# Weight pieces split in place: six high slots, low parts over the raw piece, clearing spread over the dense stage

## Time and profile before

| what | value |
|---|---|
| median of three runs | 1771.09 us (1769.48 to 1774.81) |
| the profiled execution's own time | 1762.26 us |
| its span, first to last instruction | 1760.5 us |
| mean granted TensorE clock | 0.980 |
| TensorE busy | 1648.9 us |
| VectorE busy | 1357.8 us |
| ScalarE busy | 1022.7 us |
| moved by DMA | 526.64 MB, 299 GB/s on average |

### The profile page before, as it was taken

One profiled execution on the slowest core, in us unless ns is written; L12 is line 12 of the kernel. 1 busy time (PEld: TensorE's weight loads), 2 busy tenths in 40 slices (PEclk: granted clock), 3 DMA queues, 4 the chain that ended last, 5 costly groups with the idle time before them and its releaser, 6 DMA issues.

```text
span 1760.5 us, 20788 instructions
## 1 busy us (share of the span) xinstructions
PE 1648.9 (94%) x7272; PEld 1275.6 (72%) x7273; DVE 1357.8 (77%) x1147; ACT 1022.7 (58%) x824; POOL 69.7 (4%) x85
## 2 busy tenths in 40 slices
PE   6999897999999998999999989999899999999995
PEld 2587756888587765777877768888677777787773
DVE  5687765775797776889888886565588888888888
ACT  1375432334266433778777775545577877777773
POOL 1200030000100001000000000000000000000200
PEclk9999998999999998999999999999999999999998
DMA  9885459874496445999999996666699999999992
GB/s 365 308 317 186 144 190 394 320 273 148 166 341 220 148 168 192 394 396 371 393 374 356 395 384 226 215 221 213 217 369 388 375 395 395 391 388 341 389 393 109
DMA packets 217236, 526.64 MB, mean 299 GB/s; under 512 B 9889, under 2 KB 14161, under 8 KB 217185
## 3 DMA queue, kind: packets, MB, share of 16 engines
q1 hardware_dynamic: 208770, 496.15, 77.1%
q0 software_dynamic: 8336, 29.55, 4.6%
q10 hardware_dynamic: 80, 0.26, 0.0%
HBM read 518.85 MB, written 15.47 MB: 304 GB/s over the span
## 4 chain that ended last, share of the span: by engine, by line
PE 78%; DVE 10%; issue 5%; DMA 3%; ACT 2%; ACTq 0%; DVEq 0%; SPq 0%
PE ps L1535 19%; PE ps L1537 19%; PE ps L1536 18%; PE ps L1541 5%; PE ps L1542 4%; DVE w_lo L1391 4%; PE ps L1546 4%; DMA w_raw<-in_ffn_w_dram 2%; PE ps L2036 2%; PE ps L2067 1%; DMA w_raw<-in_w_mod_mix_dram 1%; PE ps L1576 1%; ACT w_hi L814 1%; DVE gates L1170 1%; DMA w_raw<-in_w_in_dram 1%
## 5 line engine op out<-in xcount | busy, mean ns | idle before, releaser
L1391 DVE TENSOR_TENSOR w_lo<-w_raw,w_hi 128x2048 fp32r<-128x2048 f32 x333 | 756.5, 2288 | 173.4 <-ACT w_hi L814 171.1
L814 ACT CAST w_hi<-w_raw 128x2048 fp32r<-128x2048 f32 x333 | 633.6, 1910 | 178.9 <-PE ps L1542 86.9
L1535 PE MATMUL ps<-w_hi,actT_hi 128*128 128x512 f32 (+1 forms) x1464 | 583.2, 398 | 48.0 <-DVE w_lo L1391 17.3
L1537 PE MATMUL ps<-w_hi,actT_lo 128*128 128x512 f32 (+1 forms) x1464 | 569.0, 389 | 0.0
L1536 PE MATMUL ps<-w_lo,actT_hi 128*128 128x512 f32 (+1 forms) x1464 | 568.3, 388 | 0.0
L1535 PEld LDWEIGHTS ps<-w_hi,actT_hi 128*128 128x128 f32 x1464 | 278.1, 190 | 123.7 <-issue 35.0
L1537 PEld LDWEIGHTS ps<-w_hi,actT_lo 128*128 128x128 f32 x1464 | 277.8, 190 | 57.6
L1536 PEld LDWEIGHTS ps<-w_lo,actT_hi 128*128 128x128 f32 x1464 | 278.6, 190 | 53.9 <-issue 1.7
L954 DVE TENSOR_TENSOR w_lo<-w_raw,w_hi 128x2048 fp32r<-128x2048 f32 x81 | 185.4, 2289 | 104.0 <-ACT w_hi L551 103.7
L551 ACT CAST w_hi<-w_raw 128x2048 fp32r<-128x2048 f32 x81 | 154.5, 1908 | 132.4 <-PE ps L1537 91.9
L1541 PE MATMUL ps<-w_hi,gT_hi 128*128 128x512 f32 x448 | 182.3, 407 | 8.6 <-DVE gT_hi L1418 5.4
(11 more groups left out here) (281 smaller groups left out, 1204.7 us busy)
## 6 DMA issues: line engine op xcount, KB each, us to landing
w_raw<-in_exp_w_dram SPq DMA_DIRECT2D x336, 1024.0 KB, 7.6
w_raw<-in_ffn_w_dram SPq DMA_DIRECT2D x33, 1024.0 KB, 5.4
w_raw<-in_w_mod_mix_dram SPq DMA_DIRECT2D x24, 1024.0 KB, 11.4
w_raw<-in_w_mod_ffn_dram SPq DMA_DIRECT2D x24, 1024.0 KB, 5.7
w_raw<-in_w_gate_dram SPq DMA_DIRECT2D x24, 1024.0 KB, 6.7
w_raw<-in_w_in_dram SPq DMA_DIRECT2D x14, 1024.0 KB, 6.4
w_raw<-in_w_out_dram SPq DMA_DIRECT2D x8, 1024.0 KB, 5.1
by_row<-constants_dram POOLq DMA_DIRECT2D x16, 512.0 KB, 18.4
```

The source lines that it names most:

```text
L814: nc.scalar.copy(w_hi[:, i % SPLIT, :], w_raw[:, i % RING, :]).then_inc(split_hi, 1)
L1391: TTn(w_lo[:, i % SPLIT, :], w_raw[:, i % RING, :], w_hi[:, i % SPLIT, :].bitcast(F32), ALU.subtract).then_inc(piece_used, 1)
L1535: MM(to, hi, w_h, start=first, stop=False)
L1537: return MM(to, lo, w_h, start=False, stop=last)
```

## The change

`w_lo` is declared over the same memory as `w_raw`, with six slots: the subtraction writes the low part over the raw piece. `w_hi` gets six slots (SPLIT = 6), so the memory for weights stays twelve slots. SyncE now loads into a slot when TensorE has used its piece (`split_used`), or VectorE its modulation piece. Three names take over the other meanings of SPLIT: UNSPLIT (raw pieces), LAG (how far events stand behind the casts in the streams) and LATE (the last pieces of the dense stage), all 3. The rings run on from stage to stage (`first_slot`, `slot()`).

In the expert loop ScalarE and VectorE treat one piece more ahead of each event; the fourth piece of the first expert is cast and subtracted before the loop. In one-block experts a gated panel is turned after the first piece of the next panel instead of after the third, into bank 6, and the next rows are turned behind the last gated panel, into banks 2 and 3, and released in two halves. GpSimd waits for `split_used` before each clearing DMA.

```diff
-RING, SPLIT = 6, 3
+RING, SPLIT = 6, 6
+UNSPLIT = 3
+LAG = 3
+LATE = 3
...
+    def slot(self, i):
+        return (self.first_slot + i) % RING
...
+def turned_bank(blocks, b):
+    return HW1 + 2 if blocks == 1 else HW1 + 2 * b
...
-TURN_EARLY, TURN_LATE = (6, 7), (5, 7)
+TURN_FREE, TURN_LATE = (2, 3), (5, 7)
...
-        w_raw = sb("w_raw", [P, RING, PIECE])
-        w_hi = sb("w_hi", [P, SPLIT, PIECE], F32R)
-        w_lo = sb("w_lo", [P, SPLIT, PIECE], F32R)
+        w_hi = sb("w_hi", [P, SPLIT, PIECE], F32R)
+        in_place = ExitStack()
+        w_lo = sb("w_lo", [P, RING, PIECE], F32R, scope=in_place)
+        in_place.close()
+        w_raw = sb("w_raw", [P, RING, PIECE])
...
-                    if i < RING:
-                        sp.wait_ge(piece_used, base + i + 1 + (gap if i < RING // 2 else 0))
-                    elif i < RING + stretch.raw:
-                        sp.wait_ge(split_used, split_base + i - RING + 1 + SPLIT)
-                    else:
-                        sp.wait_ge(piece_used, base + i + 1 - stretch.raw)
-                    load(i % RING, piece, mod_layer if piece[0] == "mod" else layer, expert)
+                    old = before.pieces[before.n - RING + i] if i < RING else stretch.pieces[i - RING]
+                    if old[0] == "mod":
+                        sp.wait_ge(piece_used, base + i + 1 - (0 if i < RING else stretch.raw))
+                    elif i < RING:
+                        sp.wait_ge(split_used, split_base + before.split_no[before.n - RING + i] - before.n_split + 1 + SPLIT)
+                    else:
+                        sp.wait_ge(split_used, split_base + stretch.split_no[i - RING] + 1 + SPLIT)
+                    load(stretch.slot(i), piece, mod_layer if piece[0] == "mod" else layer, expert)
...
                     for n in range(EXPERTS * TT):
+                        gp.wait_ge(split_used, MIX.n_split + 3 + 3 * n // 2 + SPLIT)
                         gp.dma_start(by_row[n * P:(n + 1) * P, :], consts[:, C_ZERO:C_ZERO + D]).then_inc(rows_cleared, 16)
...
-                            round_at(3, loads0, done0)
+                            round_at(4, loads0, done0)
                             gate_of(1, done0, panel_0, fold_0, first=True)
-                            round_at(4, loads0, done0)
                             round_at(5, loads0, done0)
+                            round_at(6, loads0, done0)
                             if packed:
                                 fold_up(3, done0)
-                            round_at(6, loads0, done0)
+                            round_at(7, loads0, done0)
                             def panel(loads, done, at, folds, last):
-                                round_at(7, loads, done)
+                                if blocks == 1:
+                                    gT_part(at)
+                                round_at(8, loads, done)
                                 gate_of(5, done, at, folds)
-                                round_at(8, loads, done)
-                                gT_part(at)
                                 round_at(9, loads, done)
+                                if blocks == 2:
+                                    gT_part(at)
+                                round_at(10, loads, done)
...
                                 pe.wait_ge(silu_ready, at)
-                                up(4, "A", 0, done)
+                                up(4, "A", 0, done, turn_previous if blocks == 1 else None)
                                 up(5, "A", 1, done)
                                 pe.wait_ge(gated_ready, at)
-                                up(6, "B", 0, done, turn_previous)
+                                up(6, "B", 0, done, turn_previous if blocks == 2 else None)
...
-                            if blocks == 1:
-                                with pe.If(e < EXPERTS - 1):
-                                    turn_rows(0, e + 1, TURN_EARLY)
-                                turn(panel_0 + NP)
...
+                            turn(panel_0 + NP)
+                            with pe.If(e < EXPERTS - 1):
+                                turn_rows(0, e + 1, TURN_FREE if blocks == 1 else TURN_LATE)
+                            with pe.Else():
+                                turn_places()
```

More of the change, by code:

```diff
@@ L141, with __init__ @@
 class Stretch:
-    def __init__(self, pieces, raw=0):
-        self.pieces, self.raw = pieces, raw
+    def __init__(self, pieces, raw=0, first_slot=0):
+        self.pieces, self.raw, self.first_slot = pieces, raw, first_slot
         self.loads, self.split_no = [], []
@@ L149, in __init__ @@
         for i, piece in enumerate(pieces):
-            landed[i % RING] += 32 if piece[0] == "branch" and piece[2] == 0 else 16
-            self.loads.append(landed[i % RING])
+            landed[self.slot(i)] += 32 if piece[0] == "branch" and piece[2] == 0 else 16
+            self.loads.append(landed[self.slot(i)])
             self.split_no.append(None if piece[0] == "mod" else n)
@@ L440, in _ @@
             for layer in range(DEPTH):
-                stream(MIX, layer * LAYER_PIECES + MOD0.n_used, layer, mod_layer=("ffn", layer), gap=layer * (RING // 2),
-                       split_base=layer * LAYER_SPLITS)
+                stream(MIX, layer * LAYER_PIECES + MOD0.n_used, layer, DENSE if layer else MOD0, layer * LAYER_SPLITS, mod_layer=("ffn", layer))
                 if layer < 1:
-                    stream(DENSE, MOD0.n_used + MIX.n_used, 0, mod_layer=("mix", 1), gap=RING // 2, split_base=MIX.n_split)
+                    stream(DENSE, MOD0.n_used + MIX.n_used, 0, MIX, MIX.n_split, mod_layer=("mix", 1))
                 else:
                     moe0 = MOD0.n_used + LAYER_PIECES + MIX.n_used
-                    sp.wait_ge(piece_used, moe0 + RING)
+                    assert [piece[0] for piece in MIX.pieces[-RING:]] == ["mod"] + ["branch"] + ["out"] * (RING - 2)
+                    sp.wait_ge(piece_used, moe0 - (RING - 1) + RING)
                     with sp.Fori(0, EXPERTS) as e:
-                        stream(EXPERT, e * EXPERT.n + moe0, 1, expert=e)
+                        stream(EXPERT, None, 1, EXPERT, e * EXPERT.n_split + LAYER_SPLITS + MIX.n_split, expert=e)
             for t in range(TT):
@@ L618, in route_norms @@
                 high_h(1)
+                ahead(3)
             act.wait_ge(c_loaded, 16)
@@ L953, in rest_of_piece @@
                 dve.wait_ge(split_hi, split_base + j + 1 - RAW_UP_TO.get(split_base, RAW_PIECES))
-                TTn(w_lo[:, j % SPLIT, :], w_raw[:, i % RING, :], w_hi[:, j % SPLIT, :].bitcast(F32),
+                slot = stretch.slot(i)
+                TTn(w_lo[:, slot, :], w_raw[:, slot, :], w_hi[:, (j - stretch.raw) % SPLIT, :].bitcast(F32),
                     ALU.subtract).then_inc(piece_used, 1)
@@ L1761, in project_raw @@
                         pe.wait_ge(hT_raw_ready, layer * 8 + 2 * t + i + 1)
[L1762 removed]
+                    slot = MIX.slot(i)
+                    pe.wait_ge(raw_loaded[slot], layer * (MIX.landed[slot] + DENSE.landed[slot]) + MOD0.landed[slot] + MIX.loads[i])
                     for k in range(4 * h, 4 * h + 4):
[L1764 removed]
+                        ins = raw_product(bank(2 * t + n % 2), k, t, slot, k % 4, BANK, k == 0, k == KD - 1)
                     return ins
[L1767 removed]
+                for i in range(UNSPLIT):
                     ins = project_raw(i, 0)
@@ L1775, in _ @@
                 second_tile(layer * 2, 0)
-                for i in range(SPLIT):
+                for i in range(UNSPLIT):
                     project_raw(i, 1).then_inc(split_used, 1)
                 for i, piece in enumerate(MIX.pieces):
-                    if piece[0] == "mod" or i < SPLIT:
+                    if piece[0] == "mod" or i < UNSPLIT:
                         continue
```

211 lines of the change are left out of this document (107 added, 104 removed).

## The result

The changed kernel takes 1758.3 us (median of four runs, 1755.7 to 1760.9) against 1771.2 before (four runs as well): ratio 0.993, interval 0.991 to 0.995. The gain is 13 us, less than half of the 31.5 forecast. The profiled execution took 1755.7 us (span 1753.8), against 1762.3 (1760.5) before, so between the two traces only 6.5 us are to be found.

A forecast was written before the change was run, and what follows sets the result against it. TensorE was busy 1648.9 of 1760.5 us, leaving 112 idle plus half-clock losses. Dense stage -15.0, experts -18, mixers +1.5 gave -31.5: profiled 1730.8, median 1739.6 us, range 1722 to 1761; forecast chance 0.62.

The forecast's parts named there:

- The view of the bound, and the clearing: Dense stage: the burst of clearings fills the DMA and stalls TensorE; spreading it gives -15.0 us, ends -10 and -16.
- Two signs: Dense stage: clearings land near 3 us each; a cast waiting over 3 us for a load would refute.
- The steady panel: Experts of few rows: with six slots the DMA sets the pace, a panel going from 16.33 to 16.0 us.
- the rival that feared for it: Split-weight ring too short: loads land late, all 35 panels lengthen; 1794 or 1822 us; chance of slower 0.09.
- the clearing still collides: Dense stage rival: spread clearings take back their gain, experts gain nothing; within 5 of 1771; no change 0.05.
- Six panels per such expert -2.0.: Experts of few rows: -0.33 us a panel, six panels, so -2.0 us in each of five experts.
- The boundary: Between experts: turning the last panel first, rows behind it, wins 1.0 us with few rows, 1.5 in two TensorE-bound experts.
- Around the experts' start: Ahead of the expert loop: one more cast and subtraction lie beside TensorE's "issue" gap; 0, at most +2.3 us.
- Mixers: Mixer stages: six slots are only three split pieces there, cover 1.3 us; +1.5 us for both layers, ends -2 and +10.
- dense stage only: Rival: DMA holds the expert stage, where nothing moves; gain 10 to 20, typically 15, so 1756 us; chance 0.22.

The follow-up runs named there:

- dense_only: The kernel before, with only the clearing of the row table spread over the dense stage; 1755.2 us, ratio 0.992.
- three: Changed kernel; first panel's product behind piece 4's low part, VectorE's loop head at slot 8, piece 2's low part before the gathered rows' wait; 1743.8 us.
- slot8: Changed kernel with the head of VectorE's expert loop at slot 8 of a code block instead of slot 0; 1754.4 us, ratio 0.991.
- dense_pad: Kernel before with the spread clearing and three increments of an unused semaphore ahead of VectorE's expert loop; 1760.7 us, ratio 0.995.
- held: Changed kernel with the first expert's loads of pieces 6 and up held until VectorE is in its expert loop; 1759.0 us, ratio 0.994.
- entry: Changed kernel with VectorE's loop head at slot 8 and piece 2's low part made before the gathered rows are waited for; 1749.8 us, ratio 0.990.
- gate_first: Changed kernel; in one-block experts the first panel's gated product comes behind piece 4's low part, not piece 6's; 1755.1 us, ratio 0.992.
- rest_only: Changed kernel with the sixteen clearings issued in one burst, as before; 1774.1 us, ratio 1.003.
- all_four: `three` plus the next rows turned ahead of the last panel in one-block experts; 1749.1 us, ratio 0.988.
- three_last: `three` with the last panel's gated product made before piece 10's low part in one-block experts; 1745.6 us, ratio 0.987.
- three_pe: `three` with the head of TensorE's expert loop at slot 0 of a block of its code; 1739.5 us, ratio 0.983.

## Why the prediction was wrong

*The view of the bound, and the clearing.* Right: -15.0 forecast for the stalled piece, -14.6 measured, and `dense_only` shows it as a gain of 14.6 in the median. Two signs were wrong, and nothing hung on them: a clearing lands in 6.9 us, not near 3, and casts there wait 3.3 and 4.6 us for a load, over the 3 us that were to refute the forecast, while TensorE waits for none of them.

*The steady panel.* Right in its mechanism: 16.0 us forecast, 15.95 in the chain of the third expert, DMA at 394 GB/s, ScalarE waiting for landings, landings of 6.9 to 9.4 us. By TensorE's count of pieces 10 to 39 a panel takes 15.6 to 15.7 us in the first, third, fifth and sixth expert (16.3 before), faster than forecast, and 16.3 in the last, as before. The ring is long enough; the rival that feared for it is refuted, and so is that the clearing still collides.

*"Six panels per such expert -2.0."* The third expert shows it (-1.9), and with its early waits gone in `three` it is no faster (113.97 us, from 113.69): there its panels take 15.9 instead of 15.7, so what it lost at piece 5 it had made up behind. The last expert is 3.5 us longer instead.

*The boundary, 1.0 and 1.5 us forecast.* Half right. The low part of the rows is off TensorE's path: the first piece behind the first, fifth and sixth expert is 1.7 us shorter. But 1.3 of the 1.7 go back at piece 40, so 0.4 of the 1.0 is left, and behind the third expert, whose successor's first piece is 0.8 longer, nothing. The full experts gain 0.9 of the 1.5, at piece 40 alone: the first piece behind them took 2.8 us before, too, so the 1.45 us were never there. I counted the eight transposes as moved beside other work; before, they themselves were what covered the product on VectorE. The last expert, with no next rows, loses 2.9 (piece 40 from 3.68 to 6.54), which the forecast has no term for.

*The step that failed: "Around the experts' start ... they lie beside it: 0, at most +2.3."* Its size was +13 at piece 4; the start being 3.3 earlier and later pieces making up 2, +7.4 is left for the first expert. I took TensorE's "issue" gap as the cover and asked only what one more subtraction costs. Two things were missing. VectorE's own entry into the loop, 8.0 us of standing before, has cover only as long as TensorE starts late, and whatever makes TensorE earlier uncovers it. And the entry's length isn't fixed: two more instructions ahead of a pinned loop head (6.5 us), and weight loads issued from 677.9 us on where the old ring had none between 684 and 698 (the rest: the second further jump took 5.0 us, from 2.4). `slot8` and `dense_pad` show the first, `held` the second (both further jumps were shorter in it, 1.1 and 3.7 us), and `entry` gets 5 to 8.5 us back.

*A term that was left out: the turn of the first panel moved up.* The diff puts it behind piece 4's products instead of piece 6's, and piece 6's low part in front of the product. The forecast spoke of the ring and of the last turn and never set this wait down. Piece 5 is longer by 15.3 us over six experts; 2.8 of it are the turns themselves, which only moved there, and 12.5 the wait and the slow clock behind it. Not all of that is lost time. `gate_first` won 5.8 us in experts 2 and 7, nothing in 3 and 8. From `entry` to `three` it is 6.0 us in the median, of which the traces have 4.1 in experts 2 and 7; a part of it may be the reload that `entry`'s trace has and `three`'s hasn't.

*Mixers, +1.5 forecast.* Near: piece by piece 0.7 and 0.45 us more. Another 1.4 us came ahead of the first split piece; that is scatter, since there the new ring's traces lie from 1.4 us under before's (`rest_only`) to 1.4 over (the changed kernel itself). Seven of the eleven with the new ring lose 1.4 us more in the first mixer, which this one doesn't; why was not tried. In the eleven traces with the new ring, the last piece before the stall ends at 281.6 to 284.0, in the three with the old one at 280.5 to 281.1.

*The rival "dense stage only"* is what was measured (1756 given, 1758.3 measured), for a reason that it did not name: the transfers did move, and waits of the change's own took it back. For the entry and for the first panel's product the runs show it; for the end of an expert they show the wait, and neither edit there won time. With the first two mended the kernel is 25 us under before, of the 31.5.

## What to carry

Where a lead is won early, follow it to the next place at which an engine stands for its own code: the stand was hidden by the lateness that has just been taken away. Where a diff moves a wait forward on the consumer, look at the producer's line for what stands ahead of that result, and whether any of it waits for a load. And a stretch of transposes or other small work that "moves beside" something was perhaps itself the cover of the thing it stood before.

## What was not expected of the hardware

A loop head that the straight code misses by two instructions cost VectorE 6.4 to 7.0 us on entry, in all six traces with that layout, and 0.15 to 0.5 us in the eight others. With the new ring, each of two further jumps took 4.0 to 5.1 us with weight loads under way, and 0.9 to 2.3 in `three`, `entry`, `all_four` and `three_last`, where both began before the first of these was issued; the second took 5.4 in `three_pe`, with the row table's transfers under way instead. One idle of 2.07 us was followed by a granted TensorE clock of 0.54 for the next 3.5 us, one of 2.48 by 0.51 for 3.4; behind two of 1.02 and 1.19 us with transposes between them it stayed at 1.00. And TensorE's loading of code at the sixth expert (first piece 9.2 to 11.0 us instead of 2.7 to 4.5) comes and goes without a change in its program. The profiled run of before has none and lies 8.8 us under its median; that the other runs have it would explain this, but they carry no trace. What decides it stays open.
